# A two-layer hybrid decoder trunk in float32: four kinds of tile turned by a round trip through memory, and seven block products for eight in six pairs of gate blocks

## The reference

```python
def hybrid_layer(x, pre_g, post_g, w_in, conv_w, conv_b, w_branch_a, w_branch_c, w_branch_r, w_out):
    h = rms_norm(x, pre_g)
    proj = h @ w_in
    (q_a, k_a, v_a, z_a, u_c, b_c, c_c, z_c,
     q_r, k_r, v_r, z_r, g_a, g_c, g_r) = jnp.split(proj, cuts, axis=-1)
    ...
    o_a = o_a * jax.nn.silu(z_a)
    o_c = b_c * causal_short_conv(c_c * u_c, conv_w, conv_b) * jax.nn.silu(z_c)
    ...
    o_r = o_r * jax.nn.silu(z_r)
    merged = (jax.nn.sigmoid(g_a) * (o_a @ w_branch_a)
              + jax.nn.sigmoid(g_c) * (o_c @ w_branch_c)
              + jax.nn.sigmoid(g_r) * (o_r @ w_branch_r))
    y = merged @ w_out
    return x + rms_norm(y, post_g)
```

## Time and profile before

| | |
|---|---|
| median of 3 runs | 2746.62 us (2746.15 to 2746.77) |
| span of the profiled execution | 2743.0 us |
| TensorE busy | 2732.6 us, 12 264 matmuls |
| VectorE busy | 1924.2 us |
| ScalarE busy | 1222.0 us |
| moved by DMA | 529.10 MB, 193 GB/s on average |

### The profile page before, as it was taken

How to read it: one execution, slowest core, us unless ns; L and a number is a source line. 1 busy time by engine, 2 the same in 40 slices (tenths; PEclk the granted TensorE clock), 3 DMA queues, 4 the chain that set the end, 5 groups by cost and what they waited for, 6 DMA issues and landing times.

```text
span 2743.0 us, 30433 instructions
## 1 busy us (share of the span) xinstructions
PE 2732.6 (100%) x12264; PEld 2268.3 (83%) x12264; DVE 1924.2 (70%) x2558; ACT 1222.0 (45%) x1404; POOL 27.5 (1%) x35
## 2 busy tenths in 40 slices
PE   9999999999999999999999999999999999999998
PEld 7888888888888888888878888888888888888887
DVE  6788744777655898858567887457676558977584
ACT  6454544444443334444454545444444433434443
POOL 0000000000000000000000000000000000000000
PEclk9999999999999999999999999999999999999999
DMA  9555566565555555556575555555656565555563
GB/s 333 184 172 196 170 200 194 190 199 188 196 195 190 184 184 176 182 195 221 180 238 175 184 190 179 197 188 187 202 193 198 188 197 177 191 171 182 199 215 138
DMA packets 264732, 529.10 MB, mean 193 GB/s; under 512 B 8464, under 2 KB 8848, under 8 KB 264336
## 3 DMA queue, kind: packets, MB, share of 16 engines
q1 hardware_dynamic: 260976, 517.50, 57.4%
q10 hardware_dynamic: 2608, 4.78, 0.5%
q0 software_dynamic: 1008, 4.87, 0.5%
HBM read 522.94 MB, written 4.19 MB: 192 GB/s over the span
## 4 chain that ended last, share of the span: by engine, by line
PE 99%; DVE 0%; issue 0%; ACT 0%; DVEq 0%; POOL 0%; POOLq 0%
PE ps L651 32%; PE ps L652 32%; PE ps L653 32%; PE ps L586 0%; PE ps L606 0%; PE ps L604 0%; PE ps L603 0%; PE ps L582 0%; PE ps L567 0%; PE ps L587 0%; PE ps L581 0%; PE ps L669 0%; DVE gates L1183 0%; DVE w_trail L913 0%; DVEq L231 0%
## 5 line engine op out<-in xcount | busy, mean ns | idle before, releaser
L913 DVE TENSOR_TENSOR w_trail<-raw,w_lead 128x1024 fp32r<-128x1024 f32 x973 | 1188.7, 1225 | 763.8 <-ACT w_lead L723 754.4
L723 ACT ACTIVATE w_lead<-raw 128x1024 fp32r<-128x1024 f32 x973 | 1028.3, 1060 | 1394.1 <-PE ps L653 1387.3
L651 PE MATMUL ps<-w_lead,hT_lead 128*128 128x512 f32 x3328 | 1299.1, 390 | 0.8 <-issue 0.4
L653 PE MATMUL ps<-w_lead,hT_trail 128*128 128x512 f32 x3328 | 1295.2, 389 | 0.0
L652 PE MATMUL ps<-w_trail,hT_lead 128*128 128x512 f32 x3328 | 1295.1, 389 | 0.0
L651 PEld LDWEIGHTS ps<-w_lead,hT_lead 128*128 128x128 f32 x3328 | 625.0, 188 | 131.1 <-issue 2.2
L653 PEld LDWEIGHTS ps<-w_lead,hT_trail 128*128 128x128 f32 x3328 | 624.9, 188 | 130.0
L652 PEld LDWEIGHTS ps<-w_trail,hT_lead 128*128 128x128 f32 x3328 | 625.1, 188 | 128.4
L651 PE MATMUL ps<-w_lead,oT_lead 128*128 128x512 f32 x576 | 224.3, 389 | 0.0
L653 PE MATMUL ps<-w_lead,oT_trail 128*128 128x512 f32 x576 | 224.1, 389 | 0.0
L652 PE MATMUL ps<-w_trail,oT_lead 128*128 128x512 f32 x576 | 224.1, 389 | 0.0
(11 more groups left out here) (102 smaller groups left out, 781.7 us busy)
## 6 DMA issues: line engine op xcount, KB each, us to landing
raw<-w_in SPq DMA_DIRECT2D x381, 1024.0 KB, 5.1
raw<-w_out SPq DMA_DIRECT2D x32, 1024.0 KB, 5.0
raw<-w_branch_a SPq DMA_DIRECT2D x24, 1024.0 KB, 5.0
raw<-w_branch_c SPq DMA_DIRECT2D x24, 1024.0 KB, 5.0
raw<-w_branch_r SPq DMA_DIRECT2D x24, 1024.0 KB, 5.0
raw<-w_in SPq DMA_DIRECT2D x5, 512.0 KB, 5.0
gates<-x SPq DMA_DIRECT2D x4, 512.0 KB, 13.5
post_gain<-post_norm_g POOLq DMA_DIRECT2D x2, 1024.0 KB, 8.2
```

The source lines that it names most:

```text
L651: pe.matmul(acc, lead[:, k, tok(t)], wl, start=(k == 0), stop=False)
L653: last = pe.matmul(acc, trail[:, k, tok(t)], wl, start=False, stop=(k == BLOCKS[n][2] - 1))
L723: act.activation(w_lead[:, h % SPLIT_SLOTS, :], raw[:, i % RAW_SLOTS, part:part + HALF * COLS], ACT.Copy).then_inc(lead_ready, 1)
L913: dve.tensor_tensor(w_trail[:, s, :], raw[:, i % RAW_SLOTS, part:part + HALF * COLS], w_lead[:, s, :].bitcast(F32), ALU.subtract).then_inc ...
```

## The change

It has two parts that share buffers.

**The round trip.** q, k, z and prod are no longer turned by 16 narrow transposes. They are written by their evictions in another order of columns (`quads`), ACT then issues a DMA of the 512 KB to a scratch tensor in the chip's memory (`send_away`), two units later waits for it and issues four DMAs of 128 KB that read it back into the same tile with the rows of squares exchanged (`bring_back`; each lands in 32 partitions, in runs of 1 KB), and DVE, two to four units later, waits for these and turns the matrix by two transposes of 128 x 512 (`turn_back`). For the order to come out right, the matmuls of all mixer blocks but v read the moving weights as 16 runs of 32 columns (`columns`), 30 blocks of the 68 per layer; their output in PSUM stays contiguous. The tables of the rotation follow that order. The attention's probabilities, and the merged sum, are turned as before.

**Seven for eight.** In each mixer the gate blocks 2 and 3 form a pair (three per layer, six in all). The second half of their contraction (tiles 8 to 15) is done as before, in eight units. The first half is seen as a product of 2 x 2 matrices whose elements are blocks: two position tiles by two chunks of four contraction tiles, times two chunks by two blocks of columns. Its eight block products of 12 matmuls become seven (`PRODUCTS`), 14 units of 6 matmuls. They need sums and differences of operands: those of the activations are made once per layer (`form_work`, `form_lead_of`), those of the weights in place in `raw` by four DVE additions of 128 x 2048 per pair (`chunk_sum`). `split_lead` of the product that needs one waits for it (`summed`). p1, p6 and p7 are accumulated in one side bank, and ACT copies its state out after each (`pair_copy`); q5 has another side bank, and DVE forms two differences from it (`pair_rest_of`). The eviction of a paired gate block is then an addition on DVE and a sigmoid on ACT.

`RAW_SLOTS` goes from 4 to 5; `post_gain` shares memory with v and q and is loaded after the last retention group; `prodT` shares `probsT`; the tables of the rotation are wider (each row of them repeated per head).

```diff
-RAW_SLOTS = 4
+RAW_SLOTS = 5
...
+PAIRED_GATES = {"attention": (2,), "conv": (2,), "retention": (2,)}
...
+PRODUCTS = {"p1": ((0, 0), None), "q5": ((0, 0), (1, 0)), "p6": ((0, 0), (1, 1)), "p7": ((1, 0), (1, 1)),
+            "q3": ((1, 1), None), "p2": ((0, 1), None), "q4": ((0, 0), (0, 1))}
+PAIR_ORDER = ("p1", 0, "q5", 0, "p6", 0, "p7", 0, "q3", 1, "p2", 1, "q4", 1, 1)
+PAIR_CHUNK_ORDER = ((0, 0), (1, 0), (0, 2), (1, 1), (0, 3), (1, 2), (0, 1), (1, 3))
+
+SUM_AFTER = {"q5": "p1", "p6": "q5", "p7": "p6", "q4": "p2"}
...
 ACT_DUE = due({
-    "attention": [("exp", 4 * B + 1), ("out", 6 * B + 1)],
-    "conv": [("out", 4 * B + 6)],
-    "retention": [("square", 4 * B + 3), ("out", 5 * B + 3)]}, AHEAD)
+    "attention": [("q_away", 2 * B - 1), ("q_back", 2 * B + 1), ("k_away", 3 * B - 1), ("k_back", 3 * B + 1),
+                  ("exp", 4 * B + 1), ("z_away", 5 * B + 4), ("z_back", 5 * B + 6), ("out", 6 * B + 1)],
+    "conv": [("prod_away", 2 * B + 1), ("prod_back", 2 * B + 3), ("z_away", 4 * B + 1), ("z_back", 4 * B + 3),
+             ("out", 4 * B + 6)],
+    "retention": [("q_away", 2 * B + 1), ("q_back", 2 * B + 3), ("k_away", 3 * B + 1), ("k_back", 3 * B + 3),
+                  ("square", 4 * B + 3), ("z_away", 4 * B + 6), ("z_back", 4 * B + 8), ("out", 5 * B + 3)]}, AHEAD)
 DVE_DUE = due({
...
+    "attention": [("q", 2 * B + 4), ("k", 3 * B + 4), ("scores", 4 * B), ("sums", 4 * B + 2)]
+                 + pieces("probs", 4 * B + 3) + [("values", 5 * B + 3), ("z", 6 * B), ("out", 6 * B + 2)],
+    "conv": [("prod", 2 * B + 6), ("conv0", 2 * B + 6), ("conv1", 2 * B + 7), ("conv2", 3 * B),
+             ("gate", 4 * B), ("z", 4 * B + 6), ("product", 4 * B + 6), ("out", 4 * B + 7)],
+    "retention": [("q", 2 * B + 6), ("k", 3 * B + 5), ("scores", 3 * B + 7), ("values", 4 * B + 3),
+                  ("norm", 4 * B + 4), ("gate", 4 * B + 5), ("z", 5 * B + 2), ("out", 5 * B + 4)]}, AHEAD)
...
+PAIR_COPY_DUE = {UNIT_AT[kind, n, 1] + AHEAD: (kind, n) for n in PAIRS for kind in ("p1", "p6", "p7")}
+PAIR_REST_DUE = {UNIT_AT[kind, n, 1] + AHEAD + 1: (kind, n) for n in PAIRS for kind in ("p6", "p7")}
+SUM_DUE = {UNIT_AT[before, n, 1]: (kind, n) for n in PAIRS for kind, before in SUM_AFTER.items()}
...
+            def columns(n, ap):
+                kind, mixer, role, _j = BLOCKS[n][3]
+                if kind == "mix" and role != "v":
+                    return ap.rearrange("p (h j a) -> p j h a", h=HPB, j=QUADS)
+                return ap
...
+                elif what in SUM_AFTER and part == 0:
+                    act.wait_ge(summed, len(SUM_AFTER) * pair_no(l, n) + list(SUM_AFTER).index(what) + 1)
...
+            def send_away(l, what, mixer, g):
...
+                to = "q" if what == "prod" else what
+                act.dma_start(bounce[to], tile.rearrange("p t c -> p (t c)")).then_inc(away[to], 16)
+
+            def bring_back(l, what, mixer, g):
+
+                tile = {"q": q_sb, "prod": q_sb, "k": k_sb, "z": z_sb}[what].rearrange("p t c -> p (t c)")
+                to = "q" if what == "prod" else what
+                act.wait_ge(away[to], 16 * trips(l, to, mixer, g))
+                rows = bounce[to].rearrange("(i b) (j c) -> j b i c", i=QUADS, j=QUADS)
+                for j in range(QUADS):
+                    act.dma_start(tile[SQ * j:SQ * (j + 1), :].rearrange("b (i c) -> b i c", i=QUADS),
+                                  rows[j]).then_inc(back[to], 16)
...
+            def chunk_sum(l, what, n):
+
+                into, added = [CHUNK_LIST.index((n + i, c)) for i, c in PRODUCTS[what]]
+                dst = raw[:, SLOT_OF[l, into][0], :]
+                dve.wait_ge(*split_done(l, UNIT_AT[SUM_AFTER[what], n, CHUNK // HALF - 1]))
+                dve.wait_ge(*chunk_landed(l, into))
+                dve.wait_ge(*chunk_landed(l, added))
+                dve.tensor_tensor(dst, dst, raw[:, SLOT_OF[l, added][0], :], ALU.add).then_inc(summed, 1)
...
+                dve.wait_ge(back[to], 16 * QUADS * trips(l, to, mixer, g))
+                squares = src.rearrange("p t c -> p (t c)").rearrange("p (i t h a) -> p t h i a", i=QUADS, t=TILES, h=HPB)
+                for t in range(TILES):
+                    last = dve.transpose(dst[:, :, tok(t)].rearrange("p h (i b) -> p h i b", i=QUADS), squares[:, t])
+                last.then_inc(done, 1)
```

More of the change, by code:

```diff
@@ L75, in layer_blocks @@
                                ("mix", mixer, role, g)))
[L76 to L79, removed]
+        for kind, j in TAIL[mixer]:
+            if kind == "gate":
+                blocks.append(("w_in", COLS * (GATES_AT + OUT_BLOCKS * b + j), KT, ("gate", mixer, "", j)))
+            else:
+                blocks.append((mixer, COLS * j, KT_MIX, ("branch", mixer, "", j)))
     for j in range(OUT_BLOCKS):
@@ L118, with layer_chunks @@
-PER_BLOCK_GROUP = len(ROLES["attention"])
-MIXER_BLOCKS = PER_BLOCK_GROUP * GROUPS + 2 * OUT_BLOCKS
+        return UNITS[h]
+    i, part = (h % PAIRED, h // PAIRED) if h < CROSSED else divmod(h, CHUNK // HALF)
+    return "half", i % PAIRED, CHUNK * (i // PAIRED) + HALF * part
+def layer_chunks():
+    chunks, n = [], 0
+    while n < NBLOCKS:
+        if n in PAIRS:
+            chunks += [(n + i, c) for i, c in PAIR_CHUNK_ORDER]
+            n += 2
+        else:
+            chunks += [(n, c) for c in range(BLOCKS[n][2] // CHUNK)]
+            n += 1
+    return chunks
@@ new lines, with chunk_list, chunk_and_part, last_use @@
+CHUNK_LIST = layer_chunks()
+CHUNKS = len(CHUNK_LIST)
+PAIRED_LIST = [(i % PAIRED, i // PAIRED) for i in range(PAIR_CHUNKS)] + CHUNK_LIST[PAIR_CHUNKS:]
+def chunk_list(l):
+    return CHUNK_LIST if l else PAIRED_LIST
+def chunk_and_part(l, h):
+    kind, n, at = place(l, h)
+    if kind == "half":
+        return chunk_list(l).index((n, at // CHUNK)), at % CHUNK // HALF
+    (i, c), _added = PRODUCTS[kind]
+    return CHUNK_LIST.index((n + i, c)), at
+def last_use():
+    uses = {}
+    for l in range(DEPTH):
+        for h in range(HALVES):
+            i, _part = chunk_and_part(l, h)
+            uses[l, i] = h
+            kind, n, at = place(l, h)
+            if kind in PRODUCTS and PRODUCTS[kind][1] is not None and at == 0:
+                i, c = PRODUCTS[kind][1]
+                uses[l, CHUNK_LIST.index((n + i, c))] = h
+    return uses
@@ L123, with raw_slots @@
+LAST_USE = last_use()
+def raw_slots():
+    free_at, held, out = [None] * RAW_SLOTS, [0] * RAW_SLOTS, {}
+    for l in range(DEPTH):
+        for i in range(CHUNKS):
+            s = min(range(RAW_SLOTS), key=lambda s: (free_at[s] is not None, free_at[s] or (0, 0), s))
+            out[l, i] = s, held[s], free_at[s]
+            free_at[s] = l, LAST_USE[l, i]
+            held[s] += 1
+    return out
+SLOT_OF = raw_slots()
 AHEAD = SPLIT_SLOTS
@@ L165, with unit_after @@
 TURNS = ((0, 3), (3, 6), (6, 9), (9, 12), (12, 14), (14, 16))
+STARTS = [0]
+for _kind, _n, _at in UNITS:
+    STARTS.append(STARTS[-1] + (1 if _kind in PRODUCTS else TILES))
+def unit_after(n, at):
+    return next(h for h in range(HALVES) if STARTS[h] >= STARTS[FIRST_HALF[n]] + TILES * at)
 def due(table, offset=0):
@@ L325, in build @@
         x_mean = sem("x_mean")
+        x_pow = sem("x_pow")
         x_rstd_ready = sem("x_rstd_ready")
@@ L337, in build @@
         conv_product = sem("conv_product")
+        away = {what: sem(what + "_away") for what in ("q", "k", "z")}
+        back = {what: sem(what + "_back") for what in ("q", "k", "z")}
         q_turned = sem("q_turned")
```

511 lines of the change are left out of this document (355 added, 156 removed).

## The result

| | before | after |
|---|---|---|
| median of 4 runs each, same chip | 2746.39 us (2745.60 to 2746.77) | 2778.99 us (2778.00 to 2779.10) |
| ratio, 95% interval | | 1.0118 (1.0104 to 1.0133) |
| span of the profiled execution | 2743.0 us | 2777.1 us |

The change costs 1.2%. The forecast was 2738.7 us with a range up to 2761: wrong in sign, and the range missed it.

A forecast was written before the change was run, and what follows sets the result against it. TensorE was taken to bound the kernel, busy for all but 10 us. The span of 2743.0 us loses 16.3 and gains 8.4, 2735.1; the median, 3.6 above, is 2738.7 us, range 2729 to 2761.

The forecast's parts named there:

- What bounds the kernel: Whole kernel: TensorE at 2.4 GHz is busy for all but 10 us; time saved on the splitting engines is worth nothing.
- Reading the weights in runs of 32: 5760 matmuls of the mixer blocks but v: reading 16 runs costs 0, taken from rows of DVE.
- a cycle lost per run: Rival, same matmuls: each run costs 6.7 ns a matmul, 38 us in all, giving 2777 us; chance 0.13.
- The sign of the whole sum: Mixer block matmuls: 1.4 ns more each would eat what is left of the gain.
- Seven for eight, the saving: Six gate block pairs: each drops 12 matmuls, 2.72 us, all on the path; 16.3 us saved.
- Seven for eight, the cost: Pairs: late DVE splits lose 2.4 us in each attention pair, 0.9 in each conv or retention pair; 8.4 us.
- that tail work: Conv and retention pairs: their own tail work is done before the pair's sums, so each loses only 0.9 us.
- a late trip: Rival, retention: scores wait for k, 3.5 us in six groups, giving 2760 us, or 2749 at half; chance 0.15.
- The round trip, what it removes: DVE: 768 transposes, 335 us, become 96 of 0.70 us, 67 us; none on the path, worth 0.
- The round trip, what it adds: ACT's DMA issues and waits, 2.5 us per trip: 0, with 2.2 us of slack for retention's k; other end 21 us.
- The rule on 32 neighbouring partitions and 8 ports: Ways back: 189 GB/s, so 512 KB takes 2.8 us instead of 1.6; slack near 1 us, still no wait.
- The span and the median: Whole kernel: the median stands 3.6 us above the profiled span, so span 2735.1 gives median 2738.7 us.

The follow-up runs named there:

- e4: Kernel before, each kind of mixer block reading weights, or in three writing output, as every second run of lengths from 256 to 2 columns; 2896.51 us, one run.
- e6b: Changed kernel with weights read in one run, the order written in PSUM, and each weight sum halved around the plain unit's split; 2735.15 us, one run.
- e9: e6b with attention's turn of z moved later, between the two sums, and its out steps after that; 2734.40 us, ratio 0.9960.
- e12: e9 with ScalarE's out step of attention one unit later, behind its copy of p6, and VectorE's out behind that; 2730.42 us, ratio 0.9944.
- e2: Changed kernel with weights read in one run of 512 again, leaving the column order wrong; 2740.67 us, ratio 0.9981.
- e3: Changed kernel without the pairs, all gate blocks in 16 plain units; 2784.27 us, ratio 1.0139.
- e1: Kernel before with only the new reading order, 16 runs of 32 columns in mixer blocks but v; 2783.76 us, ratio 1.0137.
- e8: Kernel before with weights read, or output written, as every second, fourth, eighth or sixteenth run, by kind of block; 2775.29 us, one run.
- e10: Kernel before, mixer blocks reading weights and writing output in the same short order, a different one for most kinds of block; 2851.74 us, one run.
- e11: Kernel before, every matmul of 512 columns reading and writing every fourth run of 4 columns; 2740.02 us, ratio 0.9980.

## Why the prediction was wrong, step by step

**What bounds the kernel.** Right. TensorE at full clock is the bound in every kernel here; 146 us less on VectorE bought nothing that shows.

**The step that failed** is *Reading the weights in runs of 32*: "DVE reads 256 elements in four runs of 64 in 479 ns and in one run in 480, so I take 0." Measured 6.67 ns a matmul, 38.4 us. The other end of that step, a cycle lost per run, had the number to a hundredth, but by luck: in the table above the same run of 32 costs 10 ns with every second or eighth run, and eight runs of 64 cost nothing. Two things were wrong in how I chose. The row was of another engine. And it was of runs of 64, which are free on TensorE as well (226.7 in e4): the row could not tell of runs of 32. The sign of the whole sum turned at 1.4 ns, with 5760 matmuls on the critical path behind it, and a chance of 0.13 was too little for a price that no row showed.

The page I leaned on, the Trainium skill (SBUF — State Buffer, Door 1: The DMA port swizzle), says that accesses inside a 16-byte line are at full rate and each crossing to another pays; by that rule runs of 32 fill their lines and are free. The runs disagree: 233.3 and 236.7 ns against 226.7, and the measurement decides. The same skill (PSUM — Partial Sum Buffer, Specifications (TRN2)) says that any non-contiguous pattern slows matmuls significantly. Here 226.7 ns were measured for results written in runs of 32 down to 2 beside weights read in one run. The change had put the permutation on the costly side and kept the free one contiguous.

**Seven for eight, the saving.** Right: 72 matmuls, 16.3 us.

**Seven for eight, the cost.** Forecast 8.4 us, measured 9.8. In an attention pair 2.8 us against 2.4: the units are the ones named, the gaps are nearly equal (1.44 and 1.60 between starts), not 2.1 and 0.2 of delay. In conv 0.5 and 0.4 against 0.9, half of it. In retention 1.9 and 1.4 against 0.9. Two things had been left out. The out trail of retention's last group stands one unit before the first sum by its table (at 1186.08 in the trace), where the prediction held that tail work done. And the profile names a late trip. GpSimd's load of `post_gain`, then ScalarE's queue (ACTq) and its next split:

```profile
1165.94 0.61 POOL L744 DMA_DIRECT2D vq_sb<-post_norm_g  x1
```

```profile
1168.24 0.34 ACTq L1068 DMA_DIRECT2D bounce_z<-z_sb  x1
...
1175.38 2.67 ACTq L1077 DMA_DIRECT2D z_sb<-bounce_z  x4
1178.09 1.06 ACT L972 ACTIVATE w_lead<-raw 128x1024 fp32r<-128x1024 f32 x1 [6.30 <-issue]
```

z's trip out was issued at 1168.24 and took 7.1 us, where its kind has a median of 3.2; ScalarE stood in its queue for it and was idle 6.3 us before the next split. TensorE did not stop there. Its first gap comes at 1192.11, in the pair, after VectorE has worked nearly without a pause to catch up. In the second layer the trip took 7.5 us; of the other 16 trips of z none took over 3.9. The two long trips have one thing in common: each follows by 2.3 us the 1 MB load of `post_gain`, which takes 8 us and which the change moved to this place. No run moved that load, so this cause is likely and not shown. ScalarE's timeline in e6b at the same place:

```profile
1154.91 3.06 ACTq L1078 DMA_DIRECT2D z_sb<-bounce_z  x4
1158.01 2.96 ACT L973 ACTIVATE w_lead<-raw 128x1024 fp32r<-128x1024 f32 x3 [5.98 <-issue]
```

Nearly the same wait, and no gap on TensorE in retention's pair, nor in e9 and e12. With whole sums the gap grows with the delay: from the trip's issue to ScalarE's next split 8.9, 9.35 and 9.85 us (e2 and the changed kernel), largest distance of starts in the pair 0.75, 1.19 and 1.35. So a late trip cost only where sums of 2.3 us ate the margin behind it. I had priced the trips and the sums each by themselves, at 0 and 0.9.

**The round trip, what it removes.** Right: the turn of 128 x 512 took 687 ns, 702 forecast; a sum 2292 ns, 2.3 us forecast. The groups (busy us, mean ns, idle before), where the earlier trace rows had the 768 small ones:

```profile
L1506 DVE STREAM_TRANSPOSE kT<-k_sb 128x512 f32<-128x512 f32 x24 | 15.6, 687 | 0.0
L1243 DVE TENSOR_TENSOR raw<-raw 128x2048 f32<-128x2048 f32 x24 | 55.0, 2292 | 0.8
```

**The round trip, what it adds.** Right in its sum: no score matmul waited for k, and e3 less e1 is 0.5 us. The way out was quicker than counted (3.2 us for 4.6), the way back about as counted. DMA issues (KB each, median us from issue to landing):

```profile
bounce_z<-z_sb ACTq DMA_DIRECT2D x18, 512.0 KB, 3.2
z_sb<-bounce_z ACTq DMA_DIRECT2D x72, 128.0 KB, 3.4
k_sb<-bounce_k ACTq DMA_DIRECT2D x48, 128.0 KB, 4.1
```

An issue cost ScalarE 0.34 us on the way out and about 0.45 on the way back, where 0.49 was taken. The rule on 32 neighbouring partitions and 8 ports, from the Trainium skill (SBUF — State Buffer, Door 1), was set at no wait, and there was none; no run here measures the rate of such a load by itself.

**The span and the median.** I held the median 3.6 us above the span. In the changed kernel's runs it was 1.9: the profiled execution of before was one of its shorter ones. That is 1.7 us of error that has nothing to do with the change.

## What to carry to other kernels

- When the sign of a forecast hangs on a price that no row shows and the price is multiplied by thousands of instructions on the bounding engine, a row of another engine or another run length is no evidence of zero; keep the other end inside the range.
- To permute the columns of a product, read the weights in one run and let the matmul write them to their places: that was free here, and reading in runs of 32 cost 38 us. In an in-order queue beside a tight chain, halve the longest instruction, and put a step that must wait behind the short copies that free a bank.

## What the runs showed of the hardware that was not expected

- The price of reading the moving operand in runs is neither by run nor by 16 bytes: 0 ns at 128 and 64 columns, 6.7 or 10 at 32, 13 at 16, 4 to 7 at 8, 7 down to -3 at 4, 227 at 2 (e4, e8).
- Writing PSUM in runs as short as 2 columns is free beside a contiguous reading (e4, e8). With both short, 4 by 16 took 276 ns (e10); what its reading costs alone was not run.
- Runs of 4, every fourth, were read at 223.3 ns, under the 226.7 of one run, in some blocks and not in others (e8, e10, e11). This stays open.
